# Moving the mean and the centring ahead of the first residual in the last stage of a hybrid attention and convolution network

## The reference

```python
def layer_norm(x, g, b):
    mu = jnp.mean(xf, axis=-1, keepdims=True)
    var = jnp.mean(jnp.square(xf - mu), axis=-1, keepdims=True)
    y = (xf - mu) * lax.rsqrt(var + EPS)
    return y * g + b
...
    u = jax.nn.silu(layer_norm(u, g_ln, b_ln)) * jax.nn.silu(g)
    yx = u @ w_o
...
    x = x + gate_x * rms_norm(yx, g_post[i])
```

## Time and profile before

| | us |
|---|---|
| median of 3 runs | 3201.92 (3200.63 to 3202.68) |
| the profiled execution | 3201.05 |
| its span in the profile | 3199.3 |
| last stage, from its first transfer at 2940.20 | 259.1 |
| from the second `co_pvar` (block 1) to the last (block 7) | 154.75 |

### The profile page before, as it was taken

How to read it: one execution, slowest core, us unless ns; L and a number is a source line. 1 busy time by engine, 2 the same in 40 slices (tenths; PEclk the granted TensorE clock), 3 DMA queues, 4 the chain that set the end, 5 groups by cost and what they waited for, 6 DMA issues and landing times. The chain is left out here.

```text
span 3199.3 us, 44039 instructions
## 1 busy us (share of the span) xinstructions
PE 2955.6 (92%) x14979; PEld 2463.5 (77%) x14979; DVE 1778.8 (56%) x2951; ACT 1420.8 (44%) x2971; POOL 433.3 (14%) x285
## 2 busy tenths in 40 slices
PE   2999999699999999999999999797699999997698
PEld 2878878578887878788888888686588888886576
DVE  6654544367666676767676766432633333333674
ACT  3554545255655555556555565422411111112553
POOL 1000000001111111111101111000311111112331
PEclk9999999899999999999999999899799999998799
DMA  6556455511212111111111110433322222213452
GB/s 218 181 161 224 154 188 178 186 39 40 70 41 71 34 43 55 56 55 55 54 37 57 40 34 18 170 133 128 102 72 75 74 74 74 75 56 125 138 171 97
DMA packets 217948, 308.12 MB, mean 96 GB/s; under 512 B 81008, under 2 KB 142720, under 8 KB 216576
## 3 DMA queue, kind: packets, MB, share of 16 engines
q1 hardware_dynamic: 213120, 296.98, 28.7%
q10 hardware_dynamic: 4608, 8.39, 0.7%
HBM read 213.94 MB, written 91.37 MB: 95 GB/s over the span
## 5 line engine op out<-in xcount | busy, mean ns | idle before, releaser
L1086 ACT ACTIVATE at_prob<-at_S,at_nmax 128x512 f32<-128x512 f32 (+1 forms) x640 | 410.9, 658 | 371.2 <-DVE at_nmax L1200 352.8
L1223 DVE TENSOR_TENSOR at_ptlo<-at_T,at_pthi 128x512 fp32r<-128x512 f32 x576 | 396.2, 688 | 319.3 <-ACT at_pthi L1102 318.0
L1102 ACT ACTIVATE at_pthi<-at_T 128x512 fp32r<-128x512 f32 x576 | 348.8, 608 | 226.3 <-PE at_T L972 226.3
L1189 DVE TENSOR_REDUCE at_mx<-at_S 128x1 f32<-128x512 f32 (+1 forms) x640 | 392.9, 629 | 83.4 <-PE at_S L946 76.9
L972 PE MATMUL at_T<-ident,at_prob 128*128 128x128 f32 x2304 | 346.4, 273 | 1.7 <-DVE at_ptlo L1223 1.7
L972 PEld LDWEIGHTS at_T<-ident,at_prob 128*128 128x128 f32 x2304 | 279.1, 140 | 67.3 <-DVE at_ptlo L1223 14.0
L95 PE MATMUL ci_ps<-h1hi,ci_whi 128*128 128x512 f32 x768 | 300.5, 391 | 17.4 <-DVE ci_wlo L1699 17.4
L96 PE MATMUL ci_ps<-h1lo,ci_whi 128*128 128x512 f32 x768 | 300.0, 391 | 0.0
L97 PE MATMUL ci_ps<-h1hi,ci_wlo 128*128 128x512 f32 x768 | 299.8, 390 | 0.0
L941 PE MATMUL at_S<-at_khi,at_qhi 128*128 128x512 f32 (+1 forms) x640 | 250.2, 391 | 49.4 <-ACT at_prob L1086 25.6
L95 PE MATMUL at_O<-at_pthi,at_vhi 128*128 128x512 f32 x576 | 272.8, 474 | 0.6 <-DVE at_og L1232 0.5
(11 more groups left out here) (205 smaller groups left out, 6103.1 us busy)
## 6 DMA issues: line engine op xcount, KB each, us to landing
fr_w<-in_w_front SPq DMA_DIRECT2D x75, 512.0 KB, 3.9
at_wmod<-in_w_mod SPq DMA_DIRECT2D x32, 512.0 KB, 3.3
ci_w<-in_cv_w_in SPq DMA_DIRECT2D x24, 512.0 KB, 4.1
fr_w<-in_w_front SPq DMA_DIRECT2D x24, 384.0 KB, 3.8
values<-fr_ob SPq DMA_DIRECT2D x36, 256.0 KB, 2.8
at_kst<-k_nope SPq DMA_DIRECT2D x8, 1152.0 KB, 7.7
at_vst<-values SPq DMA_DIRECT2D x8, 1152.0 KB, 7.5
fr_x<-in_x SPq DMA_DIRECT2D x16, 512.0 KB, 6.7
```

The source lines that it names most:

```text
L1086: nc.scalar.activation(prob[:, j % 2, i, k], S[:, c, 0:k.stop - k.start], ACT.Exp, scale=SCALE, bias=nmax[:, i % 2:i % 2 + 1], accum_out=l ...
L1102: nc.scalar.activation(dst, T[:, (n + SLOTS * j) % 2], ACT.Copy).then_inc(s_hi, 1)
L1189: nc.vector.tensor_reduce(mx[:, i % 2, c:c + 1], S[:, c, 0:k.stop - k.start], AXX, ALU.max).then_inc(s_mx, 1)
L1223: nc.vector.tensor_tensor(ptlo[:, kt % 3], T[:, (n + SLOTS * j) % 2], pthi[:, kt % 3].bitcast(F32), ALU.subtract).then_inc(s_lo, 1)
```

## The change

In the turn of block b, `mean(b+2)` on ACT moves from behind `high(b+1)` to in front of `stat(b, 0)`. On DVE `centre(b+2)` moves from behind `low(b+1)` to in front of `residual(b, 0)`, while `square_sums(b+2)` stays behind `low(b+1)`. On PE `mean_sum(b+2)` moves from behind u=1 h=0 to behind u=0 h=1, which is 24 matmuls earlier. No instruction is added or removed.

```diff
@@ ACT, body @@
                         root(*n)
                         silu_part(*n)
+                    if not last:
+                        mean(i + 1, r)
                     stat(i, r, 0)
                     if n:
                         high(*n)
-                    if not last:
-                        mean(i + 1, r)
                     stat(i, r, 1)
@@ DVE, body @@
                         normalise(*n)
+                    if not last:
+                        centre(i + 1, r)
                     residual(i, r, 0)
                     if n:
                         low(*n)
                     if not last:
-                        centre(i + 1, r)
                         square_sums(i + 1, r)
                     residual(i, r, 1)
@@ PE, body @@
-                            if u == 1 and h == 0 and not last:
+                            if u == 0 and h == 1 and not last:
                                 mean_sum(i + 1, r)
```

## The result

The changed kernel takes 3218.93 us (median of 6 runs, 3216.11 to 3220.43), the kernel before 3203.55 us in its 6. The ratio is 1.0048, with a 95% interval of 1.0035 to 1.0061: slower by half a per cent. One of the six executions of the kernel before, 3252.37 us, is a slow one (1.6% above the fastest); the other five have a median of 3202.68, by which the ratio would be 1.0051. The forecast was 3218.5. The profiled executions are 3201.05 and 3216.11 us, their spans 3199.3 and 3214.3.

A forecast was written before the change was run, and what follows sets the result against it. The prediction took the ACT/DVE loop, held up by POOL at the SBUF port, as the bound. 3201.05 + 17.0 + 1.4 - 1.6 = 3217.9, given as 3218.5 for the median; range 3206 to 3227.

The forecast's parts named there:

- The collision with the gate: DVE's moved `centre` meets POOL's two `gate(b+1)` operations of 2.37 us; claimed to cost 3.6 us a block.
- 12.2 + 3.3 + 10.3: Us from V: `centre` may start at 12.2, undisturbed centring and squares take 3.3, the next V follows 10.3 later.
- Turns at the port: DVE and POOL alternate at the shared SBUF port: gate 11.0 to 13.35, `centre` to 14.5, gate to 16.9, `centre` to 18.0.
- The rival with one hold-up: `centre` meets the gate only once, so the next V comes at 27.1 and the time is 3207.5; chance 0.12.
- the clock: Rival: PE's clock stays half for longer, 16 more slow matmuls costing 1.6 us a block, +8, 3226; chance 0.08.
- The gain at `ob` and the loss at `normalise`: POOL's `sums` come at V + 4.25, sparing DVE's `ob` (gain 1.9 us) and holding up `normalise`, which starts at 4.3.
- V: Start of a block's `co_pvar`, PE's `var_sum(b)`, run in block b-1; the forecast counts each turn's times from it.
- S: Start of ACT's `stat(b, 0)`; forecast at V + 19.1 after the change, with the next V 10.3 us later.
- five-period term: Five periods from V(2) to V(7) grow from 25.9 to 29.3 us each: +17.0 us.
- Block 0: There `centre` is held once by the gate, and V(2) comes at 3019.5 instead of 3018.05: +1.4 us.
- the tail: PE-bound stretch from V(7), 43.52 us; its half-clock stretch (8 matmuls) now lies ahead of V(7): -1.6 us.
- A: End of ACT's silu in a turn; forecast at V + 12.4, or 13.3 if POOL came first.

The follow-up runs named there:

- Experiment 3: The changed kernel with `mu` held in PSUM instead of SBUF, same instructions, waits and order: 3201.40 us, ratio 0.9995 to the kernel before.
- experiment 4: The changed kernel with both `mu` and `rs` held in PSUM: 3194.12 us, ratio 0.9972 to the kernel before.
- experiment 6: The kernel before, order untouched, with `tmp` in PSUM so that the addition into `ob` has one SBUF input: 3193.99 us, ratio 0.9973.
- experiment 7: The changed kernel with POOL's gate reduced to 8 of 256 tokens per block, `mu` in SBUF: 3199.70 us, ratio 0.9985 to the kernel before.
- experiment 2: The kernel before with only PE's `mean_sum` moved to its new place: 3202.26 us, ratio 0.9997 to the kernel before.
- experiment 5: The kernel before, order untouched, with `mu` in PSUM, as a control: 3201.80 us, ratio 0.9991.
- experiment 9: The changed kernel with `centre` reading `pmu` directly, no `mu` copy, squares back behind `high`, `rs` in SBUF: 3184.88 us, ratio 0.9942 to the kernel before.
- experiment 8: The changed kernel with `centre` reading `pmu` directly, no `mu` copy, squares back behind `high`, `rs` in PSUM: 3182.82 us, ratio 0.9931 to the kernel before.

## Why the prediction was right

- **The bound.** The loop between ACT and DVE, not PE's share of 92%, sets the period. Experiments 3, 4 and 6 each shorten an operation of that loop and leave PE's work alone, and the period follows. PE is close behind, as the prediction's 29.7 against 29.4 had it: in three of the five turns after the change PE comes last at `co_pvar`, by 0.1 to 0.4 us.
- **The collision with the gate.** Forecast 3.6 us a block. Experiment 3 removes it by an operand's place and experiment 7 by the gate's length, for 2.8 and 2.7 us a period. Without the collision the forecast's own steps give 12.2 + 3.3 + 10.3 = 25.8, and experiment 3 has 26.0. `centre` itself takes 3.1 us longer (5.46 instead of 2.35).
- **Turns at the port.** Forecast from one place ahead of the loop: gate, half of `centre`, gate, half of `centre`. ACT's squares at 3062.98 and 3066.32, 3.34 us apart, show it. The rival with one hold-up (27.1) is out. (Where the prediction says that who is served next is the third rival, it means the second of its list. The third is the clock.)
- **The gain at `ob` and the loss at `normalise`.** Right: 1.22 at `ob`, 4.57 at the product with `rs`, which starts at V + 4.22 (forecast 4.3).
- **The sizes.** S was forecast at V + 19.1 and is at 3067.28 - 3048.78 = 18.5: the gate starts at V + 10.7 instead of 11.0, a turn at the port takes 3.34 instead of 3.5, and the last square 0.96 instead of 1.1. V follows S by 10.3 as forecast (3077.57 - 3067.28). The period was taken as 29.3 and is 28.8, so the five-period term is 14.7 instead of 17.0. Block 0 gives +1.1 (forecast 1.4), the tail -1.7 (forecast -1.6). The sum for the profiled execution was 3217.9, it took 3216.1.
- **PE's waits.** They are where they were forecast and shorter: 2.9 us in the mean for `vlo` in front of each block (forecast 3.5), 1.1 at `co_pmu` (11.05 - 9.4 = 1.65). Half clock for the nine matmuls behind the wait for `vlo` holds before the three starts of `co_pvar` at which PE comes last (granted clock 0.52 to 0.57). Before the other two it doesn't: 0.67 and 1.00.
- **PE's edit.** I called it neutral by itself, which experiment 2 bears out. That it is worth 12 us to the other two edits was not in the prediction: it put `mu`, left where it was, at V + 14.9, "behind A", and didn't follow what that would cost.

That the median came out within half a microsecond of the forecast is partly luck, as two errors cancel. The loop was forecast 2.3 us too long. And 3217.9 with 0.9 on top is 3218.8, not 3218.5, while the profiled run of the changed kernel lies 2.8 us under its median (3216.11 and 3218.93), not 0.6 or 0.9.

The Trainium skill's rule ("SBUF — State Buffer", "SBUF: two separate sides"), that a VectorE operation with two SBUF inputs and a GpSimd operation that reads SBUF exclude each other, agrees with experiments 3 to 7, also in its condition: with one input in PSUM the same operation runs beside the gate in 2.35 us instead of 5.46.

## What to carry to other kernels

Before moving a step, lay the instructions of every engine side by side for one period, and look for what POOL does where VectorE's step is to go: the order within an engine may be neutral and the overlap with another not. A small operand that is broadcast (a mean, a reciprocal root) can live in PSUM, and the operation that reads it then runs beside POOL's. A hold-up counts where it lies in the loop that sets the period, and even there not always with its whole length. With `rs` in SBUF `normalise` took 4.56 to 5.63 us in experiment 3, where it took 2.35 in experiment 4, and the period was 1.4 us longer. In experiment 9, with PE as the bound, it took 3.87 to 4.87 us, and the period was 0.2 us longer than in experiment 8.

## What the runs showed of the hardware

- VectorE's and POOL's waiting operations take strict turns, one operation each, when both have work waiting: in the timeline after, the gate's two operations take 5.73 us where they take 4.76 beside a `centre` with `mu` in PSUM, and `centre` 5.46 instead of 2.35.
- A `TENSOR_TENSOR` of 128x1024 with one operand in PSUM takes the time of one with both in SBUF: 2.35 us for two.
- The reciprocal of `rs`, with one SBUF input, isn't held: in the trace before it takes 1.74 us at 3048.77, as always, though POOL's 512-wide addition runs until 3050.00. That addition waits for `ob`, until about 3048.8, and not for the reciprocal.
- Whether TensorE's clock falls after a wait of 3 us isn't fixed. Two windows of the trace after, each from the end of a wait for `vlo` (2.93 and 2.94 us) to about the next `co_pvar`: the granted clock is 0.67 of full speed in one, so part of it lies at 1.2 GHz, and 1.00 in the other, all at 2.4 GHz.

```profile
3074.11:3078.20 4.09, 3.69 (x11) 2.46 (x12) 3.99 (x6) 0.00 (x0) 0.00 (x0) 0.67 0.97 291
3131.53:3135.30 3.77, 2.68 (x11) 1.90 (x11) 3.67 (x6) 0.00 (x0) 0.00 (x0) 1.00 0.97 291
```
